# In-chunk taps of a state-space branch in 32-column strips over lagged copies

## The reference

```python
lam_bar = jnp.exp(lam * step)
b_bar = ((lam_bar - 1.0) / lam)[..., None] * lax.complex(b_re, b_im)
bu = jnp.einsum('gnk,blgk->blgn', b_bar, ug)
bu = bu.at[:, 0].add(lam_bar * h0)
_, states = lax.associative_scan(combine, (a, bu), axis=1)     # s[t] = lam_bar * s[t-1] + bu[t]
y = jnp.real(jnp.einsum('gkn,blgn->blgk', c, states)) + d * ug
```

## Time and profile before

| | |
|---|---|
| median of 3 runs | 1071.95 us (1071.65 to 1072.99) |
| profiled execution, its span | 1076.74 us, 1075.0 us |
| busy PE, DVE, ACT, POOL | 939.4, 473.7, 335.4, 55.6 us |
| mean granted clock of TensorE | 0.928 |
| DMA | 297.70 MB, 277 GB/s over the span |

### The profile page before, as it was taken

One profiled execution on the slowest core, in us unless ns is written; L12 is line 12 of the kernel. 1 busy time (PEld: TensorE's weight loads), 2 busy tenths in 40 slices (PEclk: granted clock), 3 DMA queues, 4 the chain that ended last, 5 costly groups with the idle time before them and its releaser, 6 DMA issues.

```text
span 1075.0 us, 16048 instructions
## 1 busy us (share of the span) xinstructions
PE 939.4 (87%) x6687; PEld 632.0 (59%) x6687; DVE 473.7 (44%) x797; ACT 335.4 (31%) x672; POOL 55.6 (5%) x82
## 2 busy tenths in 40 slices
PE   8989999999999999999999999767678587677474
PEld 6778478995579999988878744323223223132121
DVE  5999945667677445556565410200102020202023
ACT  5333155566476245553444421100000000000002
POOL 2701300010100000000000000000000000000000
PEclk9989999999999999999999989968878788879798
DMA  9581450345462744524799779999999999999994
GB/s 272 138 211 47 154 197 2 119 139 172 138 211 100 303 157 151 205 80 157 262 358 355 307 311 401 430 428 427 428 427 427 429 428 429 426 427 422 427 422 154
DMA packets 82069, 297.70 MB, mean 277 GB/s; under 512 B 20030, under 2 KB 29978, under 8 KB 67533
## 3 DMA queue, kind: packets, MB, share of 16 engines
q1 hardware_dynamic: 79508, 289.30, 69.7%
q0 software_dynamic: 2112, 7.28, 2.0%
q10 hardware_dynamic: 376, 0.10, 0.0%
HBM read 286.76 MB, written 9.90 MB: 276 GB/s over the span
## 4 chain that ended last, share of the span: by engine, by line
PE 65%; DMA 25%; DVE 5%; SPq 2%; issue 1%; ACT 1%; DVEq 0%; ACTq 0%
DMA ring<-in_w_exp_down_dram 12%; PE bank L2257 7%; DMA ring<-in_w_exp_gate_dram 7%; DMA ring<-in_w_exp_up_dram 5%; PE bank L1909 5%; PE bank L1910 5%; PE bank L1911 5%; PE bank L1500 5%; PE bank L1515 5%; PE bank L2275 4%; PE bank L2303 3%; PE bank L1524 3%; PE bank L1800 2%; PE bank L1699 2%; PE bank L1920 2%; PE bank L1921 1%
## 5 line engine op out<-in xcount | busy, mean ns | idle before, releaser
L2257 PE MATMUL bank<-ring,work 128*32 128x512 f32 x704 | 141.8, 710 | 67.6 <-DMA work<-in_w_exp_up_dram 21.6
L2257 PEld LDWEIGHTS bank<-ring,work 128*32 128x32 f32 x704 | 34.9, 127 | 154.3 <-issue 122.9
L1909 PE MATMUL bank<-ops,usplit 128*128 128x320 f32 x368 | 114.5, 311 | 1.1 <-DVE usplit L2778 1.1
L1910 PE MATMUL bank<-ops,usplit 128*128 128x320 f32 x368 | 113.9, 310 | 0.0
L1911 PE MATMUL bank<-ops,usplit 128*128 128x320 f32 x368 | 113.9, 309 | 0.0
L2275 PE MATMUL bank<-ring,work 128*32 128x512 f32 x416 | 67.3, 714 | 40.2 <-DMA ring<-in_w_exp_down_dram 27.7
L2778 DVE TENSOR_TENSOR usplit<-ring,usplit 128x2048 fp32r<-128x2048 f32 x31 | 71.0, 2290 | 52.9 <-ACT usplit L1186 52.9
L3105 DVE TENSOR_TENSOR work<-bank,g 128x512 f32<-128x512 f32 x7 | 4.8, 692 | 202.0 <-PE bank L2303 202.0
L2257 PE MATMUL bank<-work 128*32 128x512 f32 x304 | 87.9, 712 | 0.0
L1515 PE MATMUL bank<-work,ring 128*128 128x320 f32 (+1 forms) x304 | 78.7, 417 | 1.1 <-issue 1.1
L1186 ACT ACTIVATE usplit<-ring 128x2048 fp32r<-128x2048 f32 x32 | 61.5, 1922 | 41.7 <-PE bank L1911 31.6
(11 more groups left out here) (513 smaller groups left out, 1648.2 us busy)
## 6 DMA issues: line engine op xcount, KB each, us to landing
ring<-in_w_exp_down_dram SPq DMA_DIRECT2D x20, 2048.0 KB, 19.9
ring<-in_w_exp_gate_dram SPq DMA_DIRECT2D x18, 2048.0 KB, 16.4
ring<-in_w_exp_up_dram SPq DMA_DIRECT2D x16, 2048.0 KB, 20.0
ring<-in_w_in_dram SPq DMA_DIRECT2D x10, 2048.0 KB, 9.9
work<-in_w_exp_up_dram SPq DMA_DIRECT2D x8, 2048.0 KB, 28.8
work<-in_w_exp_gate_dram SPq DMA_DIRECT2D x6, 2048.0 KB, 21.8
ring<-in_w_exp_gate_dram SPq DMA_DIRECT2D x11, 1024.0 KB, 7.8
ring<-in_w_glu_dram SPq DMA_DIRECT2D x4, 2048.0 KB, 8.7
```

Source lines behind the costliest of these rows:

```text
L1909: nc.tensor.matmul(b[:, 0:T], wh, hi_[:, k], start=(k == 0), stop=False)
L1910: nc.tensor.matmul(b[:, 0:T], wh, lo_[:, k], start=False, stop=False)
L2257: ins = nc.tensor.matmul(psum[part][ES * x:ES * (x + 1), :], xs[i % 2][:, kk, x], wt[x][:, k], start=(kk == 0), stop=(kk == KT - 1))
```

## The change

The in-chunk sum contracts, for each 32 features, four lags at once: 4 x 32 = 128 rows. Its moving operand `ux` holds a tile's u5 four times, each time one lag later, for four blocks of 32 features; its weights `ks` are 32 columns wide, for four column strips of the array. Two rounds of four matmuls, for lags 0 to 3 and 4 to 7, replace eight full-height ones.

SP writes u5 by tile to a second scratch, reads the lagged copies from it (four DMAs a tile, four buffers), and moves the taps, which DVE masks to pairs of groups (`lag_taps`), from the partitions of their features to those of their lag (16 DMAs). POOL zeroes the columns before each lag. The taps' matmuls move behind xbc0, all four `chunk_out` ahead of the first sum; `yT` has four buffers. xhi and xlo are made before the sums, the second half-block is rounded after them, and the xbc2 weights are loaded after the copies. Some semaphores are merged; with them DVE's wait for the two b loads becomes one for all nine loads of the S5 parameters and states (`ld_s5`).

```diff
-    j += ["xbc0", "xbc1", "dtT", "xbc2", "dt3", "xbc3"]
-    j += ["ye0", "yo0", "kk0", "ye1", "yo1"]
+    j += ["xbc0", "kk0", "kk1", "xbc1", "dtT", "xbc2", "dt3", "xbc3"]
+    for n in range(4):
+        j += [f"ye{n}", f"yo{n}"]
...
-        kbd = [view(ring[:, 17408:21504], (4, Q, P)), w(13056, 4, Q, P)]
+        tapm, ks = w(13056, Q, KT, 2 * S5K), w(15104, 4, 2, KT, 2 * S5K)
+        ux = [view(ring[:, 17408 + 4 * T * i:17408 + 4 * T * (i + 1)], (4, T)) for i in range(3)] + [w(13056, 4, T)]
...
-            for n in range(BIDX["mk1"], BIDX["z1"] + 1):
-                load_block(n)
+            def lagged_in(ft):
+                rows_of = scr_t.rearrange("(s f) (t n) -> f s t n", s=4, t=KT)
+                for lag in range(4):
+                    sp.dma_start(ux[ft % 4][32 * lag:32 * lag + 32, :, NCK * lag:T], rows_of[:, :, ft, 0:T - NCK * lag]).then_inc(
+                        s[f"ux{ft % 4}"], 16)
+            load_block(BIDX["mk1"])
+            for ft in range(KT):
+                sp.dma_start(scr_t.rearrange("p (t j c) -> p t j c", t=KT, j=Q)[:, ft], u5T[:, :, ft]).then_inc(s["u5_out"], 16)
+            load_block(BIDX["mv0"])
+            load_block(BIDX["mv1"])
+            sp.wait_ge(s["u5_out"], 16 + 16 * KT)
+            sp.wait_ge(s["uxz"], 1)
+            for ft in range(3):
+                lagged_in(ft)
+            load_block(BIDX["xbc0"])
+            load_block(BIDX["xbc1"])
+            sp.wait_ge(s["tapm"], 1)
+            for k in range(4):
+                for lag in range(4):
+                    sp.dma_start(ks[32 * lag:32 * lag + 32, k], tapm[32 * k:32 * k + 32, 3 - lag::4]).then_inc(s["s5_in"], 16)
+            sp.wait_ge(s["uxz"], 2)
+            lagged_in(3)
+            for ft in range(4, KT):
+                got(sp, f"fy{ft - 4}")
+                lagged_in(ft)
+            load_block(BIDX["xbc2"])
...
-                pe.wait_ge(s["kbd"], ft + 1)
-                for d in range(Q):
-                    ins = nc.tensor.matmul(b[:, NCK * d:T], kbd[ft // 4][:, ft % 4, Q - 1 - d], u5T[:, 0:Q - d, ft],
-                                     start=(d == 0), stop=(d == Q - 1))
+                pe.wait_ge(s["s5_in"], 16 * (Q + 16))
+                pe.wait_ge(s[f"ux{ft % 4}"], 64 * (ft // 4 + 1))
+                for late in range(2):
+                    cols = T // 2 * late
+                    for k in range(4):
+                        ins = nc.tensor.matmul(b[32 * k:32 * k + 32, cols:T], ks[:, k, 1 - late, ft], ux[ft % 4][:, k, 0:T - cols],
+                                               start=(late == 0), stop=(late == 1))
...
-            dve.wait_ge(s["ld_b"], 32)
+            dve.wait_ge(s["ld_s5"], 16 * 9)
...
+            def lag_taps(i):
+                job, sts = f"kk{i}", slice(4 * i, 4 * i + 4)
+                got(dve, job)
+                tap = bank(job)[:, :].rearrange("p (f q k) -> p q f k", f=4, q=Q)
+                for h_ in range(2):
+                    ins = TS(tapm[:, :, sts, S5K * h_:S5K * (h_ + 1)], tap, par2[:, h_:h_ + 1], None, ALU.mult)
+                emptied(ins, job)
+                done(dve, job)
+                for ft in range(4 * i, 4 * i + 4):
+                    ins = STT(out=tapm[:, Q - 1, ft], in0=fold4[:, :], scalar=vec[:, V_D5 + ft:V_D5 + ft + 1], in1=tapm[:, Q - 1, ft],
+                              op0=ALU.mult, op1=ALU.add)
+                if i:
+                    ins.then_inc(s["tapm"], 1)
```

More of the change, by code:

```diff
@@ L617, in _ @@
             for ri, name in enumerate(("s5_b_re", "s5_b_im")):
-                small(bnat[:, ri], a[name][0].rearrange("(s h) n k -> (h n) s k", h=2), "ld_b")
+                small(bnat[:, ri], a[name][0].rearrange("(s h) n k -> (h n) s k", h=2), "ld_s5")
             load_block(1)
@@ L836, in _ @@
             done(pool, "hi7")
+            pool.wait_ge(s["wrg"], 1)
+            lagged = ring[:, 17408:17408 + 12 * T].rearrange("p (a n) -> p a n", n=T)
+            for lag in range(1, 4):
+                ins = pool.memset(lagged[32 * lag:32 * lag + 32, :, 0:NCK * lag], 0.0)
+                if lag < 3:
+                    q(ins)
+            ins.then_inc(s["uxz"], 1)
+            pool.wait_ge(s["uxz"], 1)
             pool.wait_ge(s["rot"], 1)
@@ L1647, in _, with taps @@
             al = [ones[:, :], ones[:, :], same_s[:, :, :].rearrange("p b l -> p (b l)")]
+            def taps(i):
+                b = take(f"kk{i}")
+                for st in range(HST * i, HST * (i + 1)):
+                    k, f = st % 4, st // 4 % 4
+                    for ri in range(2):
+                        ins = nc.tensor.matmul(b[32 * k:32 * k + 32, P * f:P * (f + 1)],
+                                               bx[:, ri, st].rearrange("p h k -> p (h k)"),
+                                               ctab[i][:, st % HST, ri, 1:Q + 1].rearrange("p q k -> p (q k)"),
+                                               start=(ri == 0), stop=(ri == 1))
+                end(ins, f"kk{i}")
             pe.wait_ge(s["rot"], 1)
@@ L1650, in _ @@
                 proj("xbc", m, hnT, T)
+                if m == 0:
+                    for i in range(2):
+                        pe.wait_ge(s["ctab"], i + 1)
+                        taps(i)
                 if m == 1:
@@ L1680, in chunk_out @@
                                     end(ins, f"y{'eo'[h_]}{n_}")
[L1682 to L1692, removed]
             def chunk_sum(ft):
                 b = take(f"fy{ft}")
-                pe.wait_ge(s["kbd"], ft + 1)
-                for d in range(Q):
-                    ins = nc.tensor.matmul(b[:, NCK * d:T], kbd[ft // 4][:, ft % 4, Q - 1 - d], u5T[:, 0:Q - d, ft],
-                                     start=(d == 0), stop=(d == Q - 1))
-                    if d == Q - 1:
-                        end(ins, f"fy{ft}")
+                pe.wait_ge(s["s5_in"], 16 * (Q + 16))
[5 more added lines that the diff above has]
+                                               start=(late == 0), stop=(late == 1))
+                end(ins, f"fy{ft}")
                 b = take(f"ty{ft}")
@@ L1708, in chunk_sum @@
                     ins = nc.tensor.transpose(b[:, NCK * i:NCK * (i + 1)],
-                                              yT[ft // 2 % 2][rows, Q - 1 - i].rearrange("p s h k -> p (s h k)"), ident[rows, rows])
+                                              yT[ft // 2][rows, Q - 1 - i].rearrange("p s h k -> p (s h k)"), ident[rows, rows])
                 end(ins, f"ty{ft}")
-            chunk_out(0)
-            taps(0)
-            chunk_out(1)
+            for n_ in range(4):
+                chunk_out(n_)
             for ft in range(KT):
                 chunk_sum(ft)
[L1717 to L1720, removed]
             for m in range(2):
@@ L2635, in _ @@
                     TT(dte, dtx, dtm, ALU.min).then_inc(s["dtx"], 1)
[L2637 to L2654, removed]
             def chunk_outputs(ft):
```

110 lines of the change are left out of this document (57 added, 53 removed).

## The result

| | before | after |
|---|---|---|
| median of 13 runs each, taken together | 1072.99 us (1071.65 to 1076.49) | 1066.96 us (1065.88 to 1071.27) |
| ratio, 95% interval | | 0.995 [0.9936, 0.9963] |
| profiled execution, its span | 1076.74, 1075.0 us | 1071.27, 1069.5 us |

The change made the kernel 0.5% faster: 6.0 us by the medians, 5.5 by the spans. The forecast was 9.4 faster, 1062.5; the measured time lies in the whole range, 1057 to 1069, but outside the forecast's own, 1059.5 to 1065.5. The runs of both kernels fall into two groups some 4 us apart, and both profiled executions are of the upper one.

The account below looks back on a forecast made before the run. PE was taken to bound the S5 stage: 15.3 us less PE work, of which ACT's queue keeps 4.4, gives -10.9; the merged semaphore adds 1.5: -9.4, 1062.5 us. Own range 1059.5 to 1065.5, whole range 1057 to 1069.

Parts of the forecast that it names:

- the whole range: Total time between 1057 and 1069 us, with about 0.2 left outside on both sides together.
- the forecast's own: Range of the main forecast, 1059.5 to 1065.5 us, from the bounds of the sums and the semaphore; chance 0.58.
- The sums: In-chunk sums on PE: 0.91 us a tile instead of 2.82, 15.3 us less PE work, nothing charged for tiling switches.
- The ACT list: S5 stage: 16.7 us of ACT work frees the third sum's bank at 175.3; this queue keeps 4.4 of 15.3 us.
- the 4 to 5 that were to show it: Sign in the new profile: PE waits 4 to 5 us in all for ACT's bank copies in the S5 stage.
- I charge no clock: S5 stage: PE stalls on ACT under 2.2 us each were taken not to lower PE's clock; 0 us charged.
- The merged semaphore: DVE's L2517 waits for all nine S5 loads, starting near 34.3 instead of 31.77; loss 0 to 2.7, taken as 1.5 us.
- SP's queue: 56 added DMAs: scratch writes 6 to 14 us, tap moves 7.3 us to issue, lagged copies; all expected hidden.
- small writes: Rival: 160-byte scratch writes take 28 us and delay mv0, PE stands some 6 us: 1068.5 us; chance 0.07.
- dear moves: Rival: sixteen tap moves at 2.4 us each delay the first sum to 188: 1083.5 us; chance 0.07 with similar stalls.
- The lagged copies: Four copies for each later tile, 2.4 us a tile; tiles 4 to 7 land by 176.2, hidden by 3 us.
- data late: Rival: lagged copies take 4.3 us a tile, so the S5 stage ends 4.5 us later: 1067 us; chance 0.12.

Follow-up runs that it names:

- e2_dummy_matmuls: Changed kernel plus twelve dummy 128x128 matmuls on PE, three behind the second in-chunk sum and nine behind the fourth: 1061.62 us, 0.9893.
- The two pairs of runs: b loads' own semaphore against the merged wait: on the changed kernel 1068.28 against 1066.96 us, with dummy matmuls in both 1060.58 against 1061.62.
- the control: The changed kernel run again unaltered, with a second profile: 1069.59 us, 0.9958 of the kernel before.
- e1_own_b_wait: Changed kernel with the two S5 b loads counting on their own semaphore again, so DVE no longer waits for the c matrices: 1068.28 us, 0.9947.
- e3_dve_takes_half: Changed kernel with four of ACT's eight inter-chunk output copies given to DVE and the normed input's split moved behind the first output: 1065.24 us, 0.9916.

## Why the prediction was right, and the step that failed

*The sums: right.* At full clock a tile's sum takes 0.95 to 1.02 us, against 0.91 and an upper bound of 1.21; only the first takes longer, 1.37 in the changed kernel. The switches between strips and transposes show no price: a sum that starts every 1.56 to 1.57 us with 0.95 and 0.61 of work has nothing in between. The Trainium skill, "TensorEngine Tiling (Array Packing)", Key Properties, says that a change of the mode drains the engine; no piece of the trace shows time lost to it, and the 0.04 by which 0.95 exceeds the estimate leaves room for no more than that.

*The ACT list: right.* The third sum was to be out of its bank at 175.3; ACT's copy of it ends near 175.5 and the sixth sum starts at 175.63. With the clock kept, the stage takes 23.80 us (the dummies), where the forecast's own numbers give 24.06 (156.64 to 180.7), and the wait of the seventh transposes for DVE, the last in the forecast's list, is there with 0.5 us. In the changed kernel itself PE waits for ACT 2.45 us and not the 4 to 5 that were to show it, since the slow clock lengthens the sums and so hides the rest, and the key transposes start at 183.98 and not near 182.

*The step that failed: "Its stalls on PE are under 2.2 us each; the trace has the clock at half only after 4.3, so I charge no clock".* The one long wait of the trace before showed that a long stall costs the clock, and I read it as if shorter ones did not. The reading was wrong for that trace too. In the routing of the kernel before, the clock falls behind a single wait of 0.79 us:

```profile
617.71 0.31 PE L2206 MATMUL bank<-moh_r,before_r 128*128 128x96 f32 x1 [0.79 <-DVE moh_r L3035]
```

```profile
615.00:618.00 3.00, 2.21 (x9) 1.06 (x8) 2.42 (x14) 3.00 (x2) 0.00 (x0) 1.00 0.99 418
620.00:622.00 2.00, 2.00 (x7) 1.55 (x8) 1.58 (x9) 1.50 (x3) 0.00 (x0) 0.50 1.04 438
```

In the S5 stage of the changed kernel, stalls of 0.50, 0.20 and 1.75 us within 6 us were enough. Price: 26.80 less 24.06, 2.7 us in the stage, and 1.9 behind it, 4.7 together; the dummies gave back 4.9. The Trainium skill, "TensorE: Matmul & The Clock Gate", section "A second HAM failure mode: psum-queue depth-cycling", describes something close to this case: in a kernel that goes through its PSUM banks in a circle, TensorE stands still briefly and often between groups of matmuls and swings between its two clocks. The trace agrees so far as one fall goes (0.54 from 173.50 to 183.91), and each of the three stalls is a wait for a bank. I had not weighed that rule.

*The merged semaphore: right in its mechanism, hidden in the sum.* L2562 starts at 34.44 (34.3 forecast) and waits for the c matrices; PE's wait is 6.2 (5.8 forecast).

```profile
34.44 0.74 DVE L2562 TENSOR_TENSOR work<-work,s5p 128x512 f32<-128x512 f32 x1 [2.15 <-DMA ring<-in_s_c_im_dram]
```

The two pairs of runs give 0.9 and 2.3 us for the term of 1.5. But the stage begins 0.55 us later than before, not 1.5. Before has a gap of 1.1 us on PE at 84 us, put down to "issue", which the changed kernel does not have; why, no run settles.

```profile
84.43 1.08 issue
```

So 1.0 us of the expected loss is missing in the comparison, and that hides a part of the clock's price: -9.4 + 4.7 - 1.0 = -5.7, which is what the start of the split projections shows (194.66 to 188.94). That 1.0 us was luck: no term of the forecast has it.

*SP's queue: mis-sized, still hidden.* The scratch writes hold SP for 18.86 us (6 to 14 forecast), the moves of the taps 10.84 (7.3). mv0 was requested at 86.67 and needed at 106.41; the taps were there for the first sum. The rivals "small writes" and "dear moves" did not come about.

*The lagged copies: nearer than thought.* I had 3 us in hand for the last tile. In the kernel with the late softplus piece it lands 13.6 us after the first sum's end (165.01 to 178.64), not 11.1. In the changed kernel the slow clock hides that, since its last sum begins at 181.2. When ACT's list is shortened, the rival "data late" is the next wait.

The medians then put the forecast 4.5 us too low, inside the whole range and outside its own: 3.4 from the gain (6.0 for 9.4), and 1.0 because the kernel before ran at 1072.99 here and not at 1071.95.

## What to carry to other kernels

Where an edit takes much work from the engine that bounds a stage, list what then stalls it, and ask of each such stall what the clock would cost as well as its length: several short ones in a row cost twice their own time here (4.9 against 2.45 us). The length of a stall alone does not tell whether the clock will fall, so a forecast should carry both outcomes. If the stalls can't be removed, dummy matmuls in them were cheap here, and they also tell a clock loss from a plain wait. And before the next list is shortened, look for the queue just behind it: here ACT's copies, then SP's issues and the copies themselves.

## What was not expected of the hardware

- Stalls of 0.50, 0.20 and 1.75 us brought the granted clock down to 0.50 and cost 4.9 us beside their own 2.45. It fell likewise in the control and in e1_own_b_wait, whose longest stall is 1.8 us as well, and stayed at 1.00 in both kernels with the dummies in the stalls. Stalls of 0.54, 0.70 and 0.70 us, in the profiled execution of e3_dve_takes_half, left it at 1.00.
- A clock fall in the routing, 450 us later, went with the profiles of before, after, the control and e1_own_b_wait (3 us, 68.1 against 65.2), and was absent in the six others. The changed kernel and e2_dummy_matmuls have the same wait of 0.79 us ahead of it; one falls and the other does not. What decides it is open.
- Eight writes of 160 KB in pieces of 160 bytes took SP's queue 18.86 us, one of them alone 8.81, with a median landing of 5.3 us each.
